# Queries and keys of branch C turned by DMA in two-byte halves instead of by TensorE

## The chip, the cores and the metric

The kernel runs on one core of a Trainium2 chip. The metric is the device time of one execution in microseconds (us), lower is better. All data is float32; every large product is made of three passes over operands split in a high and a low part of type float32r.

## The reference, cut to what matters

Two layers; in each, four token mixers A to D run in parallel on one input projection and are merged through gates. The change lies in mixer C, latent attention with four heads of 128 + 64 features over 512 tokens:

```python
def latent_attention(c_q, c_kv, c_kr, positions, cq_g, w_uq, ckv_g, w_ukv, qn_g, kn_g):
    q = (rms_norm(c_q, cq_g) @ w_uq).reshape(b, s, MLA_HEADS, MLA_QK)      # 128 + 64 per head
    kv = (rms_norm(c_kv, ckv_g) @ w_ukv).reshape(b, s, MLA_HEADS, MLA_NOPE + MLA_V)
    k_nope, v = kv[..., :MLA_NOPE], kv[..., MLA_NOPE:]
    k = concat([k_nope, broadcast(c_kr)])
    q, k = rms_norm(q, qn_g), rms_norm(k, kn_g)
    q, k = (rope applied to the last 64 features of each)
    sc = einsum('bqhd,bkhd->bhqk', q, k) * scale      # contracts over features
    w = softmax(where(chunk mask, sc, NEG_INF));  return w @ v
```

Queries and keys come out of their projections with tokens on the partitions (the norm sums over features there), and the scores need features on the partitions. So both have to be turned: for a pair of heads, six blocks of 128 features x 512 tokens (two heads of keys, two of queries, and one block each in which the 64 rotary features of both heads lie side by side).

## The kernel before, in words

One program per engine, written out by hand, with semaphores between them; each engine runs its instructions strictly in the order of the program. Weights come in chunks of 128 x 1024 float32 through a ring of four slots (`RING = 4`), in the order of the list `ORDER`. SyncE's queue (SP) loads chunk c as soon as chunk c - 4 is used up (`load`, L391 to L397); ScalarE copies it to `w_hi` (`weights_up_to`, L971); GpSimd makes `w_lo` by subtracting (L464, L466); TensorE multiplies (`mm3`, L491 to L493). `project` is 24 matmuls of 512 columns over the eight tiles of the normed input h.

Branch C handles its heads in two pairs per layer (`pair_c(l, p)`, one function on each engine), so there are four such passages in the kernel. `ORDER` has for pair p the chunks kq, gb(d), yb(2p), gb(d+1), gb(d+2), yb(2p+1), gb(d+3), cz, cz with d = 4p. A passage on TensorE is:

1. keys and queries from chunk kq (36 matmuls), `k_ready` and the end of kq are signalled;
2. `gate_b(d)`, `branch_b(d)`: work of branch B, 24 and 12 matmuls, put there as filling;
3. `gate_b(d+1)`, `branch_b(d+1)`. `gate_b(d+1)` writes the bank that `gate_b(d)` wrote, and so first waits for `gb_tanh` of d (L747), which ScalarE signals when its tanh of that bank is done (L1113);
4. 24 transposes of 128 x 128 against the identity (L753 to L765), six banks;
5. `gate_b(d+2)` in bank 6 and `branch_b(d+2)` in bank 7 (L766, L767; the latter waits for `yb_taken` of d+1, from VectorE's L1596);
6. scores (L770), after `t_made` of the last of the six blocks (L769).

ScalarE, in the same passage: squares of keys and queries, `q_tok` copied out of PSUM (L1156), chunk kq+3 to `w_hi`, a square root for the norms (L1161), tanh of `gate_b(d)` (L1162), chunk kq+4, tanh of `gate_b(d+1)`, chunk kq+5, then the six high parts from the turned banks (L1169), chunk kq+6, tanh of `gate_b(d+2)`. VectorE: sums of squares, the rotation of the queries (L1665 to L1669), the scaled keys `k_tok`, `k_rot` (L1675 to L1682, `k_made`), `branch_b(d)` and `branch_b(d+1)` (it takes the bank as a gated value, L1596), six low parts (L1686 to L1691), `branch_b(d+2)`, then the maxima of the scores.

Of the kernel before, what the change touches and what calls it, by code (L numbers as in the profile page):

```python
# [7 lines left out]
F32 = mybir.dt.float32  # L8
F32R = mybir.dt.float32r
BF16 = mybir.dt.bfloat16  # L10
I32 = mybir.dt.int32
ALU = mybir.AluOpType
# [95 lines left out]
def after(n):  # L108

    assert n >= 0  # L110
    return n + 1
# [13 lines left out]
def build(nc, x_in, p_in, pos_in, w_in, par_in, rows_in, const_in, out):  # L125
    ctx = ExitStack()
    with ctx:
# [40 lines left out]
        def plan(start, stop, *items):  # L168
# [44 lines left out]
            *[(n, [SEQ], F32R) for n in ("kr_hi", "kr_lo", "qr_hi", "qr_lo")])  # L213
        k_sq, q_sq = plan(36, 46, ("k_sq", [TB, PAIR, P], F32), ("q_sq", [TB, PAIR, QK], F32))
        k_tok, q_tok, k_rot, q_rot = plan(
            60, 72, ("k_tok", [TB, PAIR, P], F32), ("q_tok", [TB, PAIR, P], F32),
            ("k_rot", [TB, PAIR, 2, HALF], F32), ("q_rot", [TB, PAIR, 2, HALF], F32))
        prob, pt_hi, pt_lo, sz_c, th_b, tmp = plan(
            60, 83, ("prob", [TRI], F32), ("pt_hi", [TRI], F32R), ("pt_lo", [TRI], F32R), ("sz_c", [SEQ], F32),
            ("th_b", [2, SEQ], F32), ("tmp", [SEQ], F32))  # L220
# [35 lines left out]
        def sems(names):  # L256
            return [sem(n) for n in names.split()]
# [27 lines left out]
        t_ready, t_hi_made, t_made = sems("t_ready t_hi_made t_made")  # L285
# [27 lines left out]
        def by_head(t, block):  # L313

            return t.rearrange("p (h t c) -> p h t c", h=G, t=TB)[:, :, block, :]

        def tile(t, i, n=SEQ):

# [70 lines left out]
        @block.sync  # L389
        def _(sync):  # L390
            def load(l, name):  # L391

                c = number(l, name)
                if c >= RING:
                    sync.wait_ge(slot_done[c % RING], c // RING)
                for to, part in gathered(l, name):
                    sync.dma_start(to, part).then_inc(raw_loaded[c % RING], 16)  # L397

            def load_x(d):
                sync.dma_start(tile(x, d), x_in[:, d * SEQ:(d + 1) * SEQ]).then_inc(x_loaded[d], 16)  # L400
# [81 lines left out]
        def _(pe):  # L482
# [230 lines left out]
            def pair_c(l, p):  # L713
# [39 lines left out]
                for b, t_of in enumerate((lambda t: k_tok[:, t, 0, :], lambda t: k_tok[:, t, 1, :],  # L753
                                          lambda t: k_rot[:, t], lambda t: q_tok[:, t, 0, :], lambda t: q_rot[:, t],
                                          lambda t: q_tok[:, t, 1, :])):
                    if p == 0 and b == 4:
                        pe.wait_ge(gb_tanh, after(l * KD + d + 1))
                    if p == 0 and b == 5:
                        pe.wait_ge(yb_taken, after(l * KD + d + 1))
                    for t in range(TB):  # L760
                        i = t_of(t)
                        if b in (2, 4):
                            i = i.rearrange("p h a c -> p (h a c)")
# [198 lines left out]
        def _(act):  # L962
# [180 lines left out]
            def pair_c(l, p):  # L1143
                d, head, n, lp = 4 * p, PAIR * p, l * G + PAIR * p, l * 2 + p
                kq, kb, fill = f"kq{p}", K_BANK[p], 10 - K_BANK[p]
                act.wait_ge(k_ready, after(lp))
                for b in range(2):
                    act.activation(k_sq[:, 2 * b:2 * b + 2].rearrange("p t h c -> p (t h c)"), bank(kb + b),
# [4 lines left out]
                                   ACT.Square).then_inc(q_squared, 1)  # L1153
                act.wait_ge(krr_made, after(l))
                for t in range(TB):
                    last = act.activation(q_tok[:, t], bank(t, PAIR * QK).rearrange("p (h c) -> p h c", h=PAIR)[:, :, 0:P],  # L1156
                                          ACT.Copy)
# [8 lines left out]
                for b, (o, gain) in enumerate(((kn_hi[:, 0], "kn"), (kn_hi[:, 1], "kn"), (kr_hi[:], None),  # L1166
                                               (qn_hi[:, 0], "qn"), (qr_hi[:], None), (qn_hi[:, 1], "qn"))):
                    act.wait_ge(t_ready, after(lp * 6 + b))
                    act.activation(o, bank(b), ACT.Copy, scale=col(l, gain) if gain else 1.0).then_inc(t_hi_made, 1)  # L1169
# [156 lines left out]
        def _(dve):  # L1326
# [319 lines left out]
            def pair_c(l, p):  # L1646
# [26 lines left out]
                dve.tensor_scalar(sm("rq"), sm("qk_inv", 0, 8), Q_SCALE_C, None, ALU.mult)  # L1673
                dve.tensor_scalar(sm("neg_rq"), sm("qk_inv", 0, 8), -Q_SCALE_C, None, ALU.mult)
                for b in range(2):  # L1675
                    dve.tensor_tensor(k_tok[:, 2 * b:2 * b + 2].rearrange("p t h c -> p (t h) c"),
                                      bank(kb + b).rearrange("p (u c) -> p u c", u=4),
                                      over(sm("qk_inv", 8 + 4 * b, 4), [P, 4, P], 2), ALU.mult)
                k_inv = sm("qk_inv", 8, 8).rearrange("p (t h) -> p t h", h=PAIR)
                dve.tensor_tensor(k_rot[:].rearrange("p t h a c -> p t h (a c)"),  # L1680
                                  over(krr[:].rearrange("p t a c -> p t (a c)"), wide, 2), over(k_inv, wide, 3),
                                  ALU.mult).then_inc(k_made, 1)  # L1682
                branch_b(l, d, fill + 1)
                branch_b(l, d + 1, fill + 1)

                for b, (o, h, gain) in enumerate((  # L1686
                        (kn_lo[:, 0], kn_hi[:, 0], "kn"), (kn_lo[:, 1], kn_hi[:, 1], "kn"), (kr_lo[:], kr_hi[:], None),
                        (qn_lo[:, 0], qn_hi[:, 0], "qn"), (qr_lo[:], qr_hi[:], None),
                        (qn_lo[:, 1], qn_hi[:, 1], "qn"))):
                    dve.wait_ge(t_hi_made, after(lp * 6 + b))  # L1690
                    (gained_low(o, bank(b), col(l, gain), h) if gain else low(o, bank(b), h)).then_inc(t_made, 1)  # L1691
                branch_b(l, d + 2, 7)
                maxima(n, 0)
                probabilities(n, 0)
# [274 lines left out]
```

## Time and profile before

| | us |
|---|---|
| median of 3 runs (lowest, highest) | 1358.57 (1358.22, 1361.79) |
| the profiled execution | 1358.55 |
| its span in the trace | 1356.8 |
| busy: TensorE matmul, VectorE, ScalarE, GpSimd | 1350.7, 699.5, 560.5, 606.1 |

The profile is of one execution. Times in it are us from the span's start unless marked ns. PE is TensorE matmul, PEld its weight load, DVE VectorE, ACT ScalarE, POOL GpSimd, SP SyncE. Matmuls are pipelined: a row gives the duration of one matmul, and the time that it costs the engine is the distance to the start of the next. A line such as L493 is the line of the kernel, which can be that of a helper.

### The profile page before, as it was taken

What the parts mean: (1) busy time and instruction counts of PE and PEld (TensorE: products, weight loads), DVE (VectorE), ACT (ScalarE), POOL (GpSimd) and SP (SyncE); (2) the same over time, 40 slices, a digit from 0 to 9 for tenths busy, and PEclk for the clock granted to TensorE, in tenths of its full rate; (3) what the DMA queues carried; (4) which work ended last, traced back from release to release, by engine and by line L of the source; (5) the groups of instructions that cost most, each with busy time, mean ns of one, the idle gap of its engine ahead of it and who ended that gap; (6) DMA issues with size and microseconds to landing.
All of it is one profiled execution on the core that took longest, in us unless ns stands there. A gap on an engine that the chain in (4) does not pass through costs nothing.

```text
span 1356.8 us, 16150 instructions
## 1 busy us (share of the span) xinstructions
PE 1350.7 (100%) x6401; PEld 1136.3 (84%) x6401; DVE 699.5 (52%) x1065; ACT 560.5 (41%) x870; POOL 606.1 (45%) x455
## 2 busy tenths in 40 slices
PE   9999999999999999999999999999999999999998
PEld 8788888888888888888888888888888888888887
DVE  7996445144553223265779955441445432343743
ACT  6365454255552222224444554443555322222242
POOL 3444252444434445445565542334333444544543
PEclk9999999999999999999999999999999999999999
DMA  7322222222222333323333222223222333333332
GB/s 209 92 86 94 63 79 74 90 86 85 87 79 93 93 100 102 109 93 96 99 108 94 85 94 63 78 75 97 78 79 81 90 95 104 97 93 109 100 101 95
DMA packets 68268, 126.32 MB, mean 93 GB/s; under 512 B 9040, under 2 KB 37984, under 8 KB 68192
## 3 DMA queue, kind: packets, MB, share of 16 engines
q1 hardware_dynamic: 66960, 124.72, 30.2%
q8 instruction: 51, 0.84, 0.3%
q10 hardware_dynamic: 1232, 0.55, 0.1%
q14 instruction: 25, 0.20, 0.0%
HBM read 123.15 MB, written 2.10 MB: 92 GB/s over the span
## 4 chain that ended last, share of the span: by engine, by line
PE 98%; DVE 1%; ACT 0%; issue 0%; DVEq 0%
PE ps L491 31%; PE ps L493 31%; PE ps L492 31%; PE ps L764 1%; PE ps L699 1%; PE ps L800 1%; PE ps L686 1%; PE ps L541 1%; PE ps L551 0%; DVE n_t L1453 0%; PE ps L556 0%; DVE h_lo L1336 0%; PE ps L582 0%; DVE r_b L1448 0%; PE ps L618 0%
## 5 line engine op out<-in xcount | busy, mean ns | idle before, releaser
L464 POOL TENSOR_TENSOR w_lo<-w_raw,w_hi 128x512 fp32r<-128x512 f32 x222 | 304.4, 1371 | 724.4 <-ACT w_hi L971 724.3
L491 PE MATMUL ps<-h_hi,w_hi 128*128 128x512 f32 (+1 forms) x1160 | 452.6, 390 | 1.0 <-DVE h_lo L1336 1.0
L493 PE MATMUL ps<-h_hi,w_lo 128*128 128x512 f32 (+1 forms) x1160 | 450.2, 388 | 0.0
L492 PE MATMUL ps<-h_lo,w_hi 128*128 128x512 f32 (+1 forms) x1160 | 449.9, 388 | 0.0
L971 ACT ACTIVATE w_hi<-w_raw 128x1024 fp32r<-128x1024 f32 x227 | 238.6, 1054 | 172.5 <-PE ps L493 166.5
L466 POOL TENSOR_TENSOR w_lo<-w_raw,w_hi 128x512 fp32r<-128x512 f32 x222 | 303.7, 1368 | 0.0
L491 PEld LDWEIGHTS ps<-h_hi,w_hi 128*128 128x128 f32 x1160 | 217.9, 188 | 46.6 <-DVE h_lo L1336 2.6
L493 PEld LDWEIGHTS ps<-h_hi,w_lo 128*128 128x128 f32 x1160 | 217.8, 188 | 45.1
L492 PEld LDWEIGHTS ps<-h_lo,w_hi 128*128 128x128 f32 x1160 | 217.9, 188 | 43.3
L1771 DVE SCALAR_TENSOR_TENSOR m_part<-th,ps 128x512 f32<-128x512 f32 x48 | 33.0, 687 | 237.9 <-PE ps L493 237.7
L1196 ACT ACTIVATE th<-ps 128x512 f32<-128x512 f32 x48 | 28.7, 597 | 183.5 <-PE ps L493 183.5
L491 PE MATMUL ps<-act_hi,w_hi 128*128 128x512 f32 x192 | 75.2, 392 | 0.0
L493 PE MATMUL ps<-act_hi,w_lo 128*128 128x512 f32 x192 | 74.8, 389 | 0.0
L492 PE MATMUL ps<-act_lo,w_hi 128*128 128x512 f32 x192 | 74.7, 389 | 0.0
L491 PE MATMUL ps<-m_hi,w_hi 128*128 128x512 f32 x128 | 49.8, 389 | 0.0
L492 PE MATMUL ps<-m_lo,w_hi 128*128 128x512 f32 x128 | 49.8, 389 | 0.0
L493 PE MATMUL ps<-m_hi,w_lo 128*128 128x512 f32 x128 | 49.8, 389 | 0.0
L493 PEld LDWEIGHTS ps<-act_hi,w_lo 128*128 128x128 f32 x192 | 36.0, 188 | 7.6
L492 PEld LDWEIGHTS ps<-act_lo,w_hi 128*128 128x128 f32 x192 | 36.1, 188 | 7.3
L491 PEld LDWEIGHTS ps<-act_hi,w_hi 128*128 128x128 f32 x192 | 36.1, 188 | 7.3
L1596 DVE SCALAR_TENSOR_TENSOR merged<-th_b,ps 128x512 f32<-128x512 f32 x16 | 11.0, 684 | 50.9 <-PE ps L493 50.9
L491 PE MATMUL ps<-w_hi,act_hi 128*128 128x512 f32 (+1 forms) x96 | 36.9, 384 | 0.0
(329 smaller groups left out, 1992.2 us busy)
## 6 DMA issues: line engine op xcount, KB each, us to landing
w_raw<-w_in SPq DMA_DIRECT2D x180, 512.0 KB, 3.5
w_raw<-w_in SPq DMA_DIRECT2D x92, 128.0 KB, 2.5
w_raw<-w_in SPq DMA_DIRECT2D x36, 256.0 KB, 3.0
x<-x_in SPq DMA_DIRECT2D x8, 256.0 KB, 4.1
w_raw<-w_in SPq DMA_DIRECT2D x32, 64.0 KB, 2.0
out_x<-x SPq DMA_DIRECT2D x7, 256.0 KB, 3.7
p_raw<-p_in SPq DMA_DIRECT2D x2, 512.0 KB, 4.4
w_raw<-w_in ACTq DMA_DIRECT2D x4, 128.0 KB, 3.0
```

What stands on the lines that cost most here:

```text
L464: pool.tensor_tensor(w_lo_t[s][:, 0:4, :], w_raw_t[s][:, 0:4, :], w_hi_t[s][:, 0:4, :].bitcast(F32), ALU.subtract)
L466: pool.tensor_tensor(w_lo_t[s][:, 4:8, :], w_raw_t[s][:, 4:8, :], w_hi_t[s][:, 4:8, :].bitcast(F32), ALU.subtract).then_inc(w_lo_made, 1)
L491: pe.matmul(o, a_hi, b_hi, start=first, stop=False, skip_group_check=skip)
L492: pe.matmul(o, a_hi, b_lo, start=False, stop=False, skip_group_check=skip)
L493: return pe.matmul(o, a_lo, b_hi, start=False, stop=last, skip_group_check=skip)
L541: pe.matmul(bank(t, LAT), act_hi[:, at_[t]], v_hi[:, u, 0:LAT], start=k == 0, stop=False)
L686: last = pe.matmul(ps[:, s:s + keys], q[at_, b * P:keys], k[at_, 0:keys], start=False, stop=q is qr_lo, skip_group_check=True)
L699: last = pe.transpose(ps[:, o:o + P], prob[:, i:i + P], ident[:])
L764: last = pe.transpose(ps[:, b * 512 + t * P:b * 512 + (t + 1) * P], i, ident[:])
L971: act.activation(w_hi_t[s][:, 0:n, :], w_raw_t[s][:, 0:n, :], ACT.Copy).then_inc(w_hi_made, 1)
L1196: act.activation(th[:, i % 4, :], bank(b), ACT.Tanh, scale=0.5).then_inc(g_tanh, 1)
L1771: dve.scalar_tensor_tensor(o, th[:, i % 4, :], 1.0, bank(b), ALU.add, ALU.mult).then_inc(y_taken, 1)
```

## The change

Every block is turned as two planes of two bytes. ScalarE reads a block of float32 as pairs of 16-bit numbers and writes all lower halves and then all upper halves (`split`, 1024 elements per partition); SP issues a DMA transpose of 128 partitions x 1024 two-byte elements from SBUF to SBUF (`turn`); VectorE puts the halves together again (`merge_halves`, 1024 elements). Then the high and low parts are made as before, now from SBUF. The 24 transposes on TensorE and their waits go. The six blocks are taken in the order queries, queries, rotary queries, keys, keys, rotary keys; their instructions stand at new places in the programs of ScalarE, VectorE and SP.

```diff
+        k_half, k_turned, q_half, q_turned, kr_half, kr_turned, qr_half, qr_turned = plan(
+            36, 60, ...)          # the bytes of kn_hi, kn_lo, qn_hi, qn_lo, kr_hi, kr_lo, qr_hi, qr_lo
+        def halves(t):
+            return t.bitcast(U16).rearrange("p (s u) -> p u s", u=2)
+        def planes(t):
+            return t.bitcast(U16).rearrange("p (u s) -> p u s", u=2)
+        TURNED = (q_tok 0, q_tok 1, q_rot, k_tok 0, k_tok 1, k_rot: each with its half and its turned tile)
@@ SyncE
+            def turn(lp, first):
+                for b in range(first, first + 3):
+                    sync.wait_ge(t_split, after(lp * 6 + b))
+                    if b > 2:
+                        sync.wait_ge(t_merged, after(lp * 6 + b - 3))
+                    _, half, turned = TURNED[b]
+                    sync.dma_start_transpose(turned.bitcast(U16).rearrange("p (j s) -> p j s", j=2 * TB),
+                                             half.bitcast(U16)).then_inc(t_turned[b % 3], 16)
...
+                    if name in ("yb1", "gb3", "yb3", "gb7"):
+                        turn(l * 2 + (name in ("yb3", "gb7")), 0 if name.startswith("yb") else 3)
                     if l or not (name.startswith("lat") or name == "av0"):
                         load(l, name)
@@ TensorE, pair_c
-                pe.wait_ge(k_made, after(lp))
-                pe.wait_ge(q_taken, after(lp))
-                pe.wait_ge(q_rotated, after(lp))
-                for b, t_of in enumerate((lambda t: k_tok[:, t, 0, :], ...)):
...
-                    for t in range(TB):
...
-                        last = pe.transpose(ps[:, b * 512 + t * P:b * 512 + (t + 1) * P], i, ident[:])
-                    last.then_inc(t_ready, 1)
@@ ScalarE, pair_c
+                def split(b):
+                    act.activation(planes(TURNED[b][1]), halves(flat_tok(b)), ACT.Copy).then_inc(t_split, 1)
...
                 act.activation(sm("qk_root"), sm("qk_sum"), ACT.Sqrt, bias=eps[:], scale=1.0 / QK).then_inc(qk_root, 1)
+                act.wait_ge(q_taken, after(lp))
+                split(0)
+                split(1)
+                act.wait_ge(q_rotated, after(lp))
+                split(2)
                 gate_b(l, d, fill)
                 weights_up_to(l, kq, 4)
+                act.wait_ge(k_made, after(lp))
+                for b in (3, 4, 5):
+                    split(b)
                 gate_b(l, d + 1, fill)
                 weights_up_to(l, kq, 5)
-                for b, (o, gain) in enumerate((... six blocks, keys first ...)):
-                    act.wait_ge(t_ready, after(lp * 6 + b))
-                    act.activation(o, bank(b), ACT.Copy, scale=...).then_inc(t_hi_made, 1)
+                for b, (o, gain) in enumerate((... six blocks, queries first ...)):
+                    act.wait_ge(t_merged, after(lp * 6 + b))
+                    act.activation(o, flat_tok(b), ACT.Copy, scale=...).then_inc(t_hi_made, 1)
@@ VectorE, pair_c
+                def merge_halves(b):
+                    dve.wait_ge(t_turned[b % 3], 16 * after(lp * 2 + b // 3))
+                    dve.tensor_copy(halves(flat_tok(b)), planes(TURNED[b][2])).then_inc(t_merged, 1)
+                def turned_low(b):
...
+                    dve.wait_ge(t_hi_made, after(lp * 6 + b))
+                    (gained_low(o, flat_tok(b), ...) if gain else low(o, flat_tok(b), h)).then_inc(t_made, 1)
                 branch_b(l, d, fill + 1)
+                for b in range(6):
+                    merge_halves(b)
+                    if b > 2:
+                        turned_low(b - 3)
                 branch_b(l, d + 1, fill + 1)
-                for b, (o, h, gain) in enumerate((... six blocks ...)):
-                    ...low parts from bank(b)...
+                for b in range(3, 6):
+                    turned_low(b)
                 branch_b(l, d + 2, 7)
```

The tiles `q_tok` and `k_tok` are laid out by head and then by token block, so that a block of a head is contiguous; the instructions that write them are otherwise the same.

## Rows read from the trace of the kernel before

**Rows 1.** The page: busy time of the engines, and the chain that ended last.
```profile
PE 1350.7 (100%) x6401; PEld 1136.3 (84%) x6401; DVE 699.5 (52%) x1065; ACT 560.5 (41%) x870; POOL 606.1 (45%) x455
PE 98%; DVE 1%; ACT 0%; issue 0%; DVEq 0%
```

**Rows 2.** Waits of TensorE: waiting line, releaser, us in total, times, longest.
```profile
PE ps L582 <- DVE ones L1384: 1.1, 1, 1.1
PE ps L491 <- DVE h_lo L1336: 1.0, 3, 0.4
```

**Rows 3.** Timeline of TensorE, first passage: start, duration, engine, line, operands, count.
```profile
130.15 1.03 PE L764 MATMUL ps<-ident,k_tok 128*128 128x128 f32 x8
...
132.69 0.47 PE L491 MATMUL ps<-h_hi,w_hi 128*128 128x512 f32 x1
133.00 0.39 PE L492 MATMUL ps<-h_lo,w_hi 128*128 128x512 f32 x1
133.23 0.40 PE L493 MATMUL ps<-h_hi,w_lo 128*128 128x512 f32 x1
```

**Rows 4.** Timeline of ScalarE, first passage: from the square root to the second tanh.
```profile
119.57 0.31 ACT L1161 ACTIVATE small<-small,eps 128x16 f32<-128x16 f32 x1
119.89 1.28 ACT L1113 ACT_TABLE_LOAD   x1
121.19 0.60 ACT L1113 ACTIVATE th_b<-ps 128x512 f32<-128x512 f32 x1
121.68 1.05 ACT L971 ACTIVATE w_hi<-w_raw 128x1024 fp32r<-128x1024 f32 x1
127.63 0.60 ACT L1113 ACTIVATE th_b<-ps 128x512 f32<-128x512 f32 x1 [4.89 <-PE ps L493]
```

**Rows 5.** The same tanh in the three other passages, and two copies in a row.
```profile
184.67 0.60 ACT L1113 ACTIVATE th_b<-ps 128x512 f32<-128x512 f32 x1
792.44 0.60 ACT L1113 ACTIVATE th_b<-ps 128x512 f32<-128x512 f32 x1
839.11 2.03 ACT L971 ACTIVATE w_hi<-w_raw 128x1024 fp32r<-128x1024 f32 x2
855.99 0.60 ACT L1113 ACTIVATE th_b<-ps 128x512 f32<-128x512 f32 x1
```

**Rows 6.** Timeline of TensorE: the first matmul of gate_b(d+1) in each passage.
```profile
121.84 0.50 PE L491 MATMUL ps<-h_hi,w_hi 128*128 128x512 f32 x1
186.05 0.39 PE L491 MATMUL ps<-h_hi,w_hi 128*128 128x512 f32 x1
793.31 0.40 PE L491 MATMUL ps<-h_hi,w_hi 128*128 128x512 f32 x1
857.37 0.39 PE L491 MATMUL ps<-h_hi,w_hi 128*128 128x512 f32 x1
```

**Rows 7.** Timeline of TensorE, first passage: branch_b(d+2) begins, scores begin.
```profile
138.25 0.39 PE L491 MATMUL ps<-act_hi,w_hi 128*128 128x512 f32 x1
140.97 0.39 PE L491 MATMUL ps<-kn_hi,qn_hi 128*128 128x512 f32 x1
```

**Rows 8.** Timeline of VectorE, first passage.
```profile
114.71 1.22 DVE L1650 TENSOR_REDUCE small<-k_sq 128x8 f32<-128x1024 f32 x1 [1.23 <-ACT k_sq L1148]
119.36 0.82 DVE L1669 TENSOR_TENSOR q_rot<-q_rot,q_swap 128x512 f32<-128x512 f32 x1
122.54 0.67 DVE L1680 TENSOR_TENSOR k_rot<-krr,small 128x512 f32<-128x512 f32 x1
132.83 0.68 DVE L1336 TENSOR_TENSOR kr_lo<-ps,kr_hi 128x512 fp32r<-128x512 f32 x1
```

**Rows 9.** The page's DMA issues: KB each, median us from issue to landing.
```profile
w_raw<-w_in SPq DMA_DIRECT2D x36, 256.0 KB, 3.0
out_x<-x SPq DMA_DIRECT2D x7, 256.0 KB, 3.7
```

**Rows 10.** DMA queues from 0 to 12 us: packets, MB, share of 16 engines.
```profile
q10 hardware_dynamic: 1232, 0.55, 16.5%
```

More of the change, by code:

```diff
@@ L11 @@
 I32 = mybir.dt.int32
+U16 = mybir.dt.uint16
 ALU = mybir.AluOpType
@@ L215, in build @@
         k_tok, q_tok, k_rot, q_rot = plan(
-            60, 72, ("k_tok", [TB, PAIR, P], F32), ("q_tok", [TB, PAIR, P], F32),
+            60, 72, ("k_tok", [PAIR, TB, P], F32), ("q_tok", [PAIR, TB, P], F32),
             ("k_rot", [TB, PAIR, 2, HALF], F32), ("q_rot", [TB, PAIR, 2, HALF], F32))
+        k_half, k_turned, q_half, q_turned, kr_half, kr_turned, qr_half, qr_turned = plan(
+            36, 60, *[(n, [PAIR, SEQ], F32) for n in ("k_half", "k_turned", "q_half", "q_turned")],
+            *[(n, [SEQ], F32) for n in ("kr_half", "kr_turned", "qr_half", "qr_turned")])
         prob, pt_hi, pt_lo, sz_c, th_b, tmp = plan(
@@ L284, in build @@
             "k_ready k_squared q_squared q_taken qk_var qk_root k_made q_rotated")
-        t_ready, t_hi_made, t_made = sems("t_ready t_hi_made t_made")
+        t_split, t_merged, t_hi_made, t_made = sems("t_split t_merged t_hi_made t_made")
+        t_turned = [sem(f"t_turned{b}") for b in range(3)]
         s_ready, s_max, exp_made, p_made, pt_ready, pt_hi_made, pt_made, oc_ready, oc_gated, oc_hi_made, act_c_made = sems(
@@ L315, in by_head, with flat_tok @@
             return t.rearrange("p (h t c) -> p h t c", h=G, t=TB)[:, :, block, :]
+        def halves(t):
+            return t.bitcast(U16).rearrange("p (s u) -> p u s", u=2)
+        def planes(t):
+            return t.bitcast(U16).rearrange("p (u s) -> p u s", u=2)
+        TURNED = ((q_tok[:, 0], q_half[:, 0, :], q_turned[:, 0, :]), (q_tok[:, 1], q_half[:, 1, :], q_turned[:, 1, :]),
+                  (q_rot[:], qr_half[:], qr_turned[:]),
+                  (k_tok[:, 0], k_half[:, 0, :], k_turned[:, 0, :]), (k_tok[:, 1], k_half[:, 1, :], k_turned[:, 1, :]),
+                  (k_rot[:], kr_half[:], kr_turned[:]))
+        def flat_tok(b):
+            t = TURNED[b][0]
+            return t.rearrange("p t h a c -> p (t h a c)") if b in (2, 5) else t.rearrange("p t c -> p (t c)")
         def tile(t, i, n=SEQ):
@@ L1155, in pair_c @@
                 for t in range(TB):
-                    last = act.activation(q_tok[:, t], bank(t, PAIR * QK).rearrange("p (h c) -> p h c", h=PAIR)[:, :, 0:P],
+                    last = act.activation(q_tok[:, :, t, :], bank(t, PAIR * QK).rearrange("p (h c) -> p h c", h=PAIR)[:, :, 0:P],
                                           ACT.Copy)
@@ L1161, in pair_c @@
                 act.activation(sm("qk_root"), sm("qk_sum"), ACT.Sqrt, bias=eps[:], scale=1.0 / QK).then_inc(qk_root, 1)
+                act.wait_ge(q_taken, after(lp))
[3 more added lines that the diff above has]
+                split(2)
                 gate_b(l, d, fill)
                 weights_up_to(l, kq, 4)
+                act.wait_ge(k_made, after(lp))
+                for b in (3, 4, 5):
+                    split(b)
                 gate_b(l, d + 1, fill)
                 weights_up_to(l, kq, 5)
-                for b, (o, gain) in enumerate(((kn_hi[:, 0], "kn"), (kn_hi[:, 1], "kn"), (kr_hi[:], None),
-                                               (qn_hi[:, 0], "qn"), (qr_hi[:], None), (qn_hi[:, 1], "qn"))):
-                    act.wait_ge(t_ready, after(lp * 6 + b))
-                    act.activation(o, bank(b), ACT.Copy, scale=col(l, gain) if gain else 1.0).then_inc(t_hi_made, 1)
+                for b, (o, gain) in enumerate(((qn_hi[:, 0], "qn"), (qn_hi[:, 1], "qn"), (qr_hi[:], None),
+                                               (kn_hi[:, 0], "kn"), (kn_hi[:, 1], "kn"), (kr_hi[:], None))):
+                    act.wait_ge(t_merged, after(lp * 6 + b))
+                    act.activation(o, flat_tok(b), ACT.Copy, scale=col(l, gain) if gain else 1.0).then_inc(t_hi_made, 1)
                 weights_up_to(l, kq, 6)
@@ L1675, in pair_c @@
                 for b in range(2):
-                    dve.tensor_tensor(k_tok[:, 2 * b:2 * b + 2].rearrange("p t h c -> p (t h) c"),
-                                      bank(kb + b).rearrange("p (u c) -> p u c", u=4),
-                                      over(sm("qk_inv", 8 + 4 * b, 4), [P, 4, P], 2), ALU.mult)
+                    dve.tensor_tensor(k_tok[:, :, 2 * b:2 * b + 2, :].rearrange("p h t c -> p t h c"),
+                                      bank(kb + b).rearrange("p (t h c) -> p t h c", t=2, h=PAIR),
+                                      over(sm("qk_inv", 8 + 4 * b, 4).rearrange("p (t h) -> p t h", h=PAIR),
+                                           [P, 2, PAIR, P], 3), ALU.mult)
                 k_inv = sm("qk_inv", 8, 8).rearrange("p (t h) -> p t h", h=PAIR)
@@ L1682, in pair_c @@
                                   ALU.mult).then_inc(k_made, 1)
+                def merge_halves(b):
+                    dve.wait_ge(t_turned[b % 3], 16 * after(lp * 2 + b // 3))
+                    dve.tensor_copy(halves(flat_tok(b)), planes(TURNED[b][2])).then_inc(t_merged, 1)
+                def turned_low(b):
+                    o, h, gain = ((qn_lo[:, 0], qn_hi[:, 0], "qn"), (qn_lo[:, 1], qn_hi[:, 1], "qn"),
+                                  (qr_lo[:], qr_hi[:], None), (kn_lo[:, 0], kn_hi[:, 0], "kn"),
+                                  (kn_lo[:, 1], kn_hi[:, 1], "kn"), (kr_lo[:], kr_hi[:], None))[b]
+                    dve.wait_ge(t_hi_made, after(lp * 6 + b))
+                    (gained_low(o, flat_tok(b), col(l, gain), h) if gain else low(o, flat_tok(b), h)).then_inc(t_made, 1)
                 branch_b(l, d, fill + 1)
+                for b in range(6):
+                    merge_halves(b)
+                    if b > 2:
+                        turned_low(b - 3)
                 branch_b(l, d + 1, fill + 1)
[L1686 to L1691, printed above, removed]
+                for b in range(3, 6):
+                    turned_low(b)
                 branch_b(l, d + 2, 7)
```

10 lines of the change are left out of this document (removed).

## The prediction

> **What bounds the kernel now.** I read the page first: TensorE is busy for 1350.7 us of a span of 1356.8, and the chain that ended last lies on it for 98% [rows 1]. Then TensorE's waits: they add up to 2.1 us in two rows, all there are [rows 2]. So every us taken from TensorE's instructions is a us of the end, as long as nothing new makes it wait; and every us that it is made to wait is lost, for no reserve exists. Nothing else in the profile is near. ScalarE is at 41% on average, but the average doesn't say who is late in a passage. So next the timeline of one passage on TensorE, ScalarE and VectorE, and there the place where they meet: `gate_b(d+1)` starts on TensorE at 121.84 [rows 6], and the tanh that frees its bank ends at 121.19 + 0.60 = 121.79 [rows 4]. Its ScalarE program is dense from the square root on: root 119.57 to 119.88, table load to 121.17, tanh 121.19. In this passage ScalarE has 0.05 us to spare, and that is what the change works on.
>
> **What is taken away.** The 24 transposes start at 130.15 and the next product at 132.69: 2.54 us. The first matmul behind them takes 0.31 to the next start (132.69 to 133.00), an ordinary one 0.23 (133.00 to 133.23) [rows 3]: 0.08 more that goes. 2.62 us for each of four passages, 10.5 us, all on the path. The k_made, q_taken and q_rotated waits that go too ended long before (k_made at 123.21 [rows 8] against 130.15) and are worth nothing. The reads of PSUM in the six high and low parts become reads of SBUF: no credit, they are off the path.
>
> **What is added on ScalarE, ahead of the first tanh.** Three splits of 1024 elements. The trace has no copy of two-byte elements. The nearest row is the copy of 1024 four-byte elements: 1.05 us alone, 2.03 for two, so the second adds 0.98 [rows 4, 5]. I take 0.98. Lower bound: 0.49, if what counts are the 512 four-byte words in it. Upper bound: 1.30, a third more, for elements that lie two bytes wide with gaps; no row excludes it. A gain from them is excluded, since they are new instructions on an engine that has no gap there. Three splits: 2.94 us. Their inputs are there: q_rot is ready at 119.36 + 0.82 = 120.18 [rows 8] and the third split would start at 121.84.
>
> So the tanh ends 2.94 us later, and TensorE can start `gate_b(d+1)` at that time plus about 0.05 for the signal (what the first passage shows: 121.79 to 121.84). In the four passages the tanh ended at 121.79, 185.27, 793.04, 856.59 [rows 4, 5] and `gate_b(d+1)` started at 121.84, 186.05, 793.31, 857.37 [rows 6]. New stalls: 121.79 + 2.99 - 121.84 = 2.94; 185.27 + 2.99 - 186.05 = 2.21; 793.04 + 2.99 - 793.31 = 2.72; 856.59 + 2.99 - 857.37 = 2.21. Sum 10.1 us. That eats the gain: -10.5 + 10.1 = -0.4.
>
> **The other three splits** (keys) stand behind the tanh and chunk kq+4. First passage, new times: tanh ends at 124.73, chunk kq+4 to 125.7, k_made long there, splits end at 126.7, 127.7, 128.7. The second tanh waits for the end of gb(d+1), 127.63 + 2.94 = 130.6, so these three lie in a gap that was 4.89 us wide [rows 4]. Free, with 2 us left.
>
> **What is added on VectorE.** Six merges of 1024 elements. The nearest row is the reduction of 1024 elements, 1.22 [rows 8]; I take 1.1 (0.3 to 1.3), 6.6 us. They lie in a gap between branch_b(d) and branch_b(d+1), but now `branch_b(d+1)` stands behind the sixth merge, and TensorE's `branch_b(d+2)` waits for its `yb_taken`.
>
> **The chain through the DMA, and its deadline.** TensorE reached `branch_b(d+2)` at 138.25 and the scores at 140.97 [rows 7]. In the new order, 2.62 earlier by the transposes and 2.94 later by the stall: 138.6 and 141.3. Call T5 the landing of the sixth transfer. Then the merge (1.1), a low part (0.65; a row of this kind has 0.68 [rows 8]) and branch_b(d+1) (0.7): yb_taken at T5 + 2.5. So T5 has to be at most 136.1. The scores need two or three more low parts, T5 + 4.5, within 2.7 us of the product between: they are not the tighter one. Two paths lead to T5. From the keys: the last split ends at 128.7, which leaves 7.4 us for one transfer. From the queries: turn(3 to 5) each wait for the merge of the block three before, whose transfer starts no earlier than 120.9, 121.9, 122.9 (splits of the queries); with a transfer of L us, T5 = 122.9 + L + 1.1 + L, which is in time up to L = 6.0. And if the transfers run one after another, s us each, T5 = 120.9 + 6 s, in time up to s = 2.5.
>
> No row shows a transpose by DMA. The nearest rows are ordinary transfers of the same 256 KB: 3.0 us to land into SBUF, 3.7 out of it [rows 9], and transfers of SP overlap. By these L is 3 to 4 and the chain is hidden, at no cost. The other bound comes from small pieces: 1232 packets took 16.5% of 16 engines for 12 us, 25.7 ns each [rows 10]. One block has 1024 runs of 256 bytes; as packets, 64 on each engine, 1.6 us. If the turning cuts runs eight times finer, to 32 bytes, it is 13 us for each transfer. A gain is excluded. I take the value next to the 256 KB rows, hidden, with the weaker confidence that this deserves.
>
> The Trainium skill (VectorE: DVE Perf Modes, The three transpose paths) has 1309 ns for a 128 x 128 block by the DMA crossbar against 390 ns on TensorE, and advises TensorE where PSUM will do as the destination. Taken as a rate, eight blocks in a transfer make 10.5 us and T5 = 183.9, an estimate from that page that would cost 48 us per passage; as a time that mostly isn't rate, nothing changes. The same skill (DMA: Bandwidth & Descriptors, Latency and other measured facts) has 261 GB/s for DMA transposes, 1.0 us for a block. The two pages disagree tenfold; no row here decides.
>
> **SP's queue.** The turns stand ahead of the loads of yb(2p+1) and gb(d+3). The first was issued at 119.1 as soon as gb(d) was used up; now it waits for the third split, 122.9. It must be landed, copied (1.05) and subtracted (2.5) by `branch_b(d+2)`, 138.6: landed by 135.0, with 3.1 for the load issued by 131.9. Nine us of slack; free if a turn holds SP for under 3 us. gb(d+3) must wait for yb(2p) to be used up (about 133.1) in any case; turn(5) has passed before.
>
> **Sum.** 1358.55 (the profiled execution, 0.02 below the median of 1358.57; its span 1356.8 and 1.75 around it) - 10.5 + 10.1 + 0 = 1358.2. With splits at 1.30 it is +3.9 = 1362.1; at 0.49, 3 x 0.49 less per passage, 5.9 less = 1352.3.
>
> **Rivals.**
> - *The chain is late by a few us.* The transfers run one after another at 3.0 us [rows 9]: T5 = 138.9, 2.8 us late in each passage, 11 us: 1369. It decides from s = 2.5 on. For it: all six are issued by one queue, and each of the last three waits for a merge three before it. Against: ordinary transfers overlap. This is the case that ends slower; it covers 1362 to 1382.
> - *Transposing by DMA is slow in itself*, the page's first figure or pieces of 32 bytes. At 5 us each T5 = 150.9, 14.8 us late, 59 us: 1417. At 13 us, 200.4, 64 us late: 1615. For it: two-byte elements are scattered across partitions. Against: nothing in the trace, which shows no such operation.
> - *Splits are cheap*, 0.49 each: 1352, faster. For it: the bytes are half those of the copy. Against: ScalarE's rows scale with elements, 0.60 for 512 and 1.05 for 1024 [rows 4].
>
> **How the numbers follow.** Chain hidden, splits at 0.9 to 1.3: 0.40, 1354 to 1362, forecast 1358. Cheap splits: 0.11. Chain late by up to 6 us a passage: 0.28. Slow transposes: 0.21. What this measurement can tell from no change is about 0.3%, 4.1 us. Faster by more 0.11, within 0.40, slower by more 0.49. The range: from the cheap splits' time, 1352, with half of that case left out below it, up to 1400, which takes a third of the slow case and leaves out 0.14. More likely than not the result isn't faster, though the single likeliest time is no change.
>
> **What the profile would show.** Right: no L764; a new wait of TensorE at L491 for ScalarE's th_b, four times, 2.2 to 2.9 us; the split rows at about 1.0 us; VectorE's merges started before 135 in the first passage; no wait for yb_taken or t_made. The late chain: TensorE waits for `merged` (VectorE) ahead of `branch_b(d+2)`, and VectorE's merge for the DMA. Slow transposes: the same with tens of us, SP blocked, and w_hi waiting for DMA. What would make it wrong: a transfer over 6 us or a split far from 1 us, or a lower granted clock of TensorE behind the new pauses.

## The result and the profile after

| | us | ratio to before, 95% interval |
|---|---|---|
| before, median of 4 runs (lowest, highest) | 1359.08 (1358.22, 1361.79) | |
| the change, median of 4 runs | 1366.79 (1364.94, 1366.99) | 1.0052 (1.0037 to 1.0067) |
| spans of the profiled executions | 1356.8 and 1364.9 | |

The change is slower by half a per cent. The forecast of no change was wrong: 1358 was forecast and 1366.8 measured, inside the stated range (1352 to 1400) and above the 4.1 us that the prediction still took for no change.

The page of the changed kernel, its busy times and the chain that ended last (answers to rows 1):

```profile
PE 1345.8 (99%) x6305; PEld 1128.5 (83%) x6305; DVE 739.4 (54%) x1089; ACT 584.3 (43%) x894; POOL 613.0 (45%) x455
PE 89%; DVE 6%; ACT 4%; issue 0%; DVEq 0%
```

96 transposes (24 in each of four passages) are gone, but TensorE's busy time fell by 4.9 us only, not by 10.5: matmuls elsewhere took longer. And 10% of the chain now lies on VectorE and ScalarE. TensorE's waits (answers to rows 2; waiting line, releaser, us in total, times, longest):

```profile
PE ps L526 <- ACT th_b L1132: 9.1, 4, 2.7
PE ps L526 <- DVE kr_lo L1367: 3.8, 4, 1.0
PE ps L617 <- DVE ones L1415: 1.1, 1, 1.1
PE ps L526 <- DVE h_lo L1367: 1.0, 3, 0.4
```

The first is the wait for the tanh that the prediction worked out. The second is new to it: the scores wait for the last low part. Next the timelines of the first passage, ScalarE, then VectorE, then SP's transposes (they answer to rows 4 and 8):

```profile
119.89 0.31 ACT L1184 ACTIVATE small<-small,eps 128x16 f32<-128x16 f32 x1
120.10 1.99 ACT L1167 ACTIVATE q_half<-q_tok 128x1024 uint16<-128x1024 uint16 x2
122.00 1.04 ACT L1167 ACTIVATE qr_half<-q_rot 128x1024 uint16<-128x1024 uint16 x1
123.06 1.28 ACT L1132 ACT_TABLE_LOAD   x1
124.35 0.60 ACT L1132 ACTIVATE th_b<-ps 128x512 f32<-128x512 f32 x1
...
132.39 0.60 ACT L1132 ACTIVATE th_b<-ps 128x512 f32<-128x512 f32 x1 [3.66 <-PE ps L528]
132.88 1.05 ACT L990 ACTIVATE w_hi<-w_raw 128x1024 fp32r<-128x1024 f32 x1
133.83 1.33 ACT L1200 ACTIVATE qn_hi<-q_tok,par 128x512 fp32r<-128x512 f32 x2
```
```profile
131.49 0.76 DVE L1718 COPY k_tok<-k_turned 128x1024 uint16<-128x1024 uint16 x1 [1.71 <-DMA k_turned<-k_half]
134.58 1.29 DVE L1371 SCALAR_TENSOR_TENSOR qn_lo<-q_tok,par,qn_hi 128x512 fp32r<-128x512 f32 x1 [2.33 <-ACT qn_hi L1200]
135.79 1.84 DVE L1718 COPY k_tok<-k_turned 128x1024 uint16<-128x1024 uint16 x1
...
139.41 0.67 DVE L1627 SCALAR_TENSOR_TENSOR merged<-th_b,ps 128x512 f32<-128x512 f32 x1
140.01 2.45 DVE L1371 SCALAR_TENSOR_TENSOR kn_lo<-k_tok,par,kn_hi 128x512 fp32r<-128x512 f32 x2
142.38 1.77 DVE L1367 TENSOR_TENSOR kr_lo<-k_rot,kr_hi 128x512 fp32r<-128x512 f32 x1
```
```profile
q_turned<-q_half SPq DMA_TRANSPOSE x8, 3.3
k_turned<-k_half SPq DMA_TRANSPOSE x8, 3.9
qr_turned<-qr_half SPq DMA_TRANSPOSE x4, 3.2
kr_turned<-kr_half SPq DMA_TRANSPOSE x4, 3.2
```

(The last four are from the page's DMA issues: count, median us to landing.) The splits cost what they were given, 1.99 for two and 1.04 for one. The DMA lands in 3.2 to 3.9 us, like an ordinary transfer of 256 KB [rows 9]. VectorE is where the surprise is: from 134.58 on it has no gap until the low part that the scores wait for is done at 144.15, and its rows are up to 2.6 times as long as the row of the same line and tile in rows 8 (1.77 against 0.68). GpSimd subtracts at the same time, and the rows of the two engines take turns:

```profile
134.01 1.30 POOL L499 TENSOR_TENSOR w_lo<-w_raw,w_hi 128x512 fp32r<-128x512 f32 x1 [4.85 <-ACT w_hi L990]
135.26 1.76 POOL L501 TENSOR_TENSOR w_lo<-w_raw,w_hi 128x512 fp32r<-128x512 f32 x1
```

VectorE's low part of 134.58 ends at 135.87, some 0.6 us behind the end of GpSimd's first row (135.31). GpSimd's second row ends 1.15 us behind that (137.02), and VectorE's merge of 135.79 ends 0.6 us behind GpSimd (137.63).

Third, the clock. Stretches of the first passage on TensorE, with the granted clock behind the busy times (stretch, length, busy time and count of PE, PEld, DVE, ACT, POOL, clock, DMA share, GB/s):

```profile
119.40:125.00 5.60, 2.86 (x13) 2.05 (x11) 4.09 (x9) 5.56 (x8) 2.25 (x2) 1.00 0.47 89
125.00:129.00 4.00, 4.00 (x11) 3.14 (x12) 4.00 (x4) 3.73 (x4) 3.03 (x2) 0.57 0.80 208
129.00:132.20 3.20, 3.20 (x16) 2.62 (x15) 1.49 (x2) 0.00 (x0) 0.16 (x1) 1.00 1.20 199
```

For 4 us behind the pause of 2.74 us the granted clock was 0.57, in the main the lower of its two levels (1.2 GHz instead of 2.4), and a matmul of 512 columns came every 0.43 us instead of 0.23.

Counted from one start to the next on TensorE's timeline, the four passages (from the start of `gate_b(d)` to the start of the scores) went like this:

| passage | before | after | `branch_b(d)` and pause | `gate_b(d+1)` | second pause |
|---|---|---|---|---|---|
| 1 | 27.39 | 30.31 | 2.72 + 2.90 | 7.19 | 1.14 |
| 2 | 27.16 | 27.90 | 2.72 + 2.10 | 5.58 | 1.12 |
| 3 | 27.18 | 30.03 | 2.72 + 2.64 | 7.18 | 1.13 |
| 4 | 27.16 | 27.89 | 2.72 + 2.11 | 5.57 | 1.13 |

Ordinary durations are 2.72 for 12 matmuls and 5.44 to 5.59 for 24. So: -10.5 for the transposes, +9.8 for the first pauses, +3.2 for the slow clock (7.19 and 7.18 against 5.58), +4.5 for the second pauses and +0.5 for the first matmul of the scores behind them (0.12 four times), 7.5 together. The spans differ by 8.1. Another 0.3 is the first matmul behind the pauses of passages 2 and 4 (`gate_b(d+1)` took 5.58 and 5.57 there, 5.44 before), and 0.3 arose ahead of the first passage.

### The profile page after: what moved, and what is told of

Same layout as the page of the kernel before. It is cut to its first block, busy times and chain, and to the rows that moved or that the text cites. A ratio compares the mean times of both kernels' runs of the same rounds, so it can differ in the third digit from the quotient of the medians.

```text
span 1364.9 us, 16038 instructions
## 1 busy us (share of the span) xinstructions
PE 1345.8 (99%) x6305; PEld 1128.5 (83%) x6305; DVE 739.4 (54%) x1089; ACT 584.3 (43%) x894; POOL 613.0 (45%) x455
## 3 DMA queue, kind: packets, MB, share of 16 engines
q1 hardware_dynamic: 92304, 131.02, 32.5%
## 4 chain that ended last, share of the span: by engine, by line
PE 89%; DVE 6%; ACT 4%; issue 0%; DVEq 0%
PE ps L526 28%; PE ps L528 28%; PE ps L527 28%; DVE kn_lo L1371 1%; ACT w_hi L990 1%; PE ps L734 1%; PE ps L819 1%; PE ps L721 1%; DVE k_tok L1718 1%; DVE qn_lo L1371 1%; DVE kr_lo L1367 0%; PE ps L576 0%; PE ps L586 0%; ACT q_sq L1175 0%; DVE n_t L1484 0%; ACT q_half L1167 0%
## 5 line engine op out<-in xcount | busy, mean ns | idle before, releaser
L499 POOL TENSOR_TENSOR w_lo<-w_raw,w_hi 128x512 fp32r<-128x512 f32 x222 | 306.2, 1379 | 725.5 <-ACT w_hi L990 725.4
L501 POOL TENSOR_TENSOR w_lo<-w_raw,w_hi 128x512 fp32r<-128x512 f32 x222 | 309.2, 1393 | 0.0
L1141 ACT ACTIVATE prob<-ps,small 128x512 f32<-128x512 f32 (+3 forms) x32 | 19.5, 614 | 44.9 <-DVE small L1644 44.9
L1315 ACT ACTIVATE o_sq<-x 128x512 f32<-128x512 f32 x16 | 10.1, 634 | 64.0 <-DVE x L1843 64.0
```

Source lines behind the costliest of these rows:

```text
L499: pool.tensor_tensor(w_lo_t[s][:, 0:4, :], w_raw_t[s][:, 0:4, :], w_hi_t[s][:, 0:4, :].bitcast(F32), ALU.subtract)
L501: pool.tensor_tensor(w_lo_t[s][:, 4:8, :], w_raw_t[s][:, 4:8, :], w_hi_t[s][:, 4:8, :].bitcast(F32), ALU.subtract).then_inc(w_lo_made, 1)
L1141: last = act.activation(prob[:, s], ps[:, sc + s.start:sc + s.stop], ACT.Exp, bias=sm("bias", h * TB + b), scale=sm("rq", b * PAIR + h), a ...
```

## The experiments

**Theory 1**: the time is lost in the order of the instructions on ScalarE and VectorE. The splits ahead of the first tanh hold up TensorE, the pause takes its clock down, and VectorE's chain of merges and low parts, lengthened by GpSimd, ends late. The DMA is not a cause. **Theory 2**, in its variants: the transposing DMA is slow or disturbs the loads; or one engine's order alone is the cause.

### The DMA replaced: e1_plain_copy

```diff
-                    sync.dma_start_transpose(turned.bitcast(U16).rearrange("p (j s) -> p j s", j=2 * TB), half.bitcast(U16))
+                    sync.dma_start(turned.bitcast(U16), half.bitcast(U16))
```

> The changed kernel, with each of its 24 DMA transposes replaced by a plain DMA copy of the same 256 KB (so queries and keys are not turned, and the scores are other numbers). Theory 1, the time is lost in the order of ScalarE and VectorE and not in the DMA: the profile of the changed kernel has TensorE wait 9.1 us for the tanh and 3.8 us for the last low part, and VectorE waits only 5.1 us for the DMA, ahead of a wait for ScalarE that ends later anyway. So no change: 1366.8, within 2 us, and the same two waits of TensorE. Theory 2, the crossbar is slow or disturbs the loads of the weights: the second wait goes and the time falls by 4 to 8 us, to 1359 to 1363.

Measured: 1365.51 (ratio to before 1.0046, 1.0031 to 1.0061), the same two waits of TensorE to the tenth of a us:

```profile
PE ps L525 <- ACT th_b L1131: 9.1, 4, 2.7
PE ps L525 <- DVE kr_lo L1366: 3.8, 4, 1.0
```

The plain copies were quicker: they landed in 2.2 to 2.4 us and held SP's queue for 0.47 us each, against 3.1 to 5.0 and 1.2 to 2.1 us for the transposes, and VectorE's 5.1 us of waits for `k_turned` are gone. The time can't be told apart from the changed kernel's all the same. So that these transfers transpose is not the cause. The transfers themselves and their place in SP's queue are still there in this run; e9 changes the order in that queue.

### The splits alone: e2_three_splits and e3_two_splits

```diff
                 act.activation(sm("qk_root"), ...).then_inc(qk_root, 1)
+                act.wait_ge(q_taken, after(lp))
+                act.wait_ge(q_rotated, after(lp))
+                for to, t in (...three blocks...)[0:3]:          # e3: [0:2]
+                    act.activation(to as two planes, t as two-byte halves, ACT.Copy)
                 gate_b(l, d, fill)
```

> The kernel before with three splits of 1024 two-byte elements on ScalarE ahead of the first tanh of a passage, and nothing else of the change: their result is not used. Theory 1: TensorE waits for the tanh in each of the four passages, 2.9 + 2.2 + 2.7 + 2.2 = 10.0 us, and behind the two longer waits its granted clock falls for some 4 us, 1.7 us each, as the trace of the changed kernel has it at 125 us: 1359.1 + 10.0 + 3.4 = 1372.5. If the clock fell for the DMA traffic or the work of VectorE and not for the wait, it stays up here: 1369.1. Theory 2: the same wait, no word on the clock.

> The kernel before with two such splits. Waits of 1.95 + 1.2 + 1.75 + 1.2 = 6.1 us. If the clock falls only behind a longer wait, as in the changed kernel behind 2.7 us and not behind 2.1 us, the granted clock stays full: 1359.1 + 6.1 = 1365.2. If any new wait made it fall, 1.7 us more for each of four: 1372.

Measured: 1377.08 (1.0132, 1.0115 to 1.0149) with three, 1368.03 (1.0063, 1.0048 to 1.0078) with two. TensorE's waits for the tanh were 11.1 and 7.3 us. They are longer than expected because my edit waits for the rotated queries ahead of all splits (ScalarE stood 0.39 us there), and because a pause costs some 0.2 us more than the wait row says, from the end of one matmul stream to the next. The rest is the clock. Two stretches of 4 us of e2, directly behind two of its pauses:

```profile
192.20:196.20 4.00, 3.94 (x10) 3.12 (x11) 0.69 (x1) 0.95 (x2) 2.51 (x2) 0.57 0.00 0
125.40:129.40 4.00, 3.98 (x17) 3.29 (x18) 0.68 (x1) 0.91 (x1) 2.54 (x2) 1.00 0.02 4
```

This kernel transposes on TensorE and moves nothing extra by DMA, and it has the slow clock too: behind three of its four pauses, `gate_b(d+1)` took 7.18, 8.31 and 7.21 us instead of 5.6. So the slow clock comes with the pauses, and it needs neither DMA traffic (0.00 in the slow stretch) nor VectorE's added work. But which pause is not settled by its length: here the longest, 3.23 us, kept the full clock and one of 2.44 did not; in e3 one of 2.29 did not and one of 2.02 did. The expectation that e3 would stay clear of it was wrong (one drop). The whole price of the three splits ahead of the tanh, as measured here, is 18.5 us.

### What could be had at most: e4_no_turning

The transposes are left out on TensorE, ScalarE waits for `k_made`, `q_taken` and `q_rotated` in their stead.

> The kernel before with the 24 transposes of a passage left out on TensorE: the high and low parts are made of what lies in the banks, so the scores are other numbers. It measures what the change could bring at most on TensorE. By the rows of before, 4 x 2.62 = 10.5 us: 1348.6. If the wait for the scores' operands became visible once the cover of 2.62 us is gone, less, some 1350 to 1353.

Measured: 1348.14 (0.992, 0.9905 to 0.9935), 10.5 us below the 1358.61 of before in the same session. The gain on TensorE was rated right. That it fits to the tenth is luck in part: the interval of the ratio allows 8.8 to 12.9 us.

### The queries' splits behind the tanh: e5_splits_behind

```diff
-                split(0); split(1); wait q_rotated; split(2)
                 gate_b(l, d, fill)
                 weights_up_to(l, kq, 4)
+                split(0); split(1); wait q_rotated; split(2)
                 act.wait_ge(k_made, after(lp))
```

> The changed kernel with one move on ScalarE: the three splits of the queries stand behind the first tanh and chunk kq+4 instead of ahead of them. Theory 1: the wait of TensorE for the tanh (10.0 us with its restarts) and the slow clock behind two of them (3.3 us) go; but then TensorE comes to branch_b(d+2) 2.6 us earlier than in the kernel before, while VectorE takes branch_b(d+1) only behind six merges, and those come with the DMA 1 to 2 us later than now. By adding up its rows yb_taken comes some 3.4 us late in each passage: 1358.6 - 10.5 + 13.6 = 1361.7, 1358 to 1366, and the wait is for VectorE's merged. Theory 2, the order of ScalarE is the whole cause: 1366.8 - 13.3 = 1353.5.

Measured: 1374.26 (1.011, 1.0096 to 1.0124), slower than the change. Both theories missed. The wait for the tanh is gone, as said, and the wait for `merged` is there, as theory 1 said, but it is 16.2 us:

```profile
PE ps L526 <- DVE merged L1627: 16.2, 4, 4.9
PE ps L526 <- DVE kr_lo L1367: 1.0, 1, 1.0
```

I had added up VectorE's rows and left out the other engine that feeds them. ScalarE, first passage:

```profile
128.90 0.58 ACT L1132 ACTIVATE th_b<-ps 128x512 f32<-128x512 f32 x1
132.64 1.06 ACT L990 ACTIVATE w_hi<-w_raw 128x1024 fp32r<-128x1024 f32 x1 [3.16 <-DMA w_raw<-w_in]
133.61 1.32 ACT L1200 ACTIVATE qn_hi<-q_tok,par 128x512 fp32r<-128x512 f32 x2
```

The chunk yb(2p+1) is loaded behind three turns in SP's queue, the turns now start at 124.3, and ScalarE stands 3.16 us for it ahead of the high parts. The pauses then bring the clock down as well: behind those of 4.17, 3.55 and 4.94 us the 12 matmuls of `branch_b(d+2)` took 4.19, 4.35 and 4.73 us instead of 2.72, with granted clocks of 0.64, 0.64 and 0.50 in the first 4 us. Behind the fourth, 3.59 us, the clock stayed at 1.00.

### VectorE without GpSimd beside it: e6_pool_quiet

```diff
+                    if name[0:2] in ("gb", "yb", "cz"):
+                        pool.memset(w_lo_t[s][:].bitcast(F32), 0.0).then_inc(w_lo_made, 1)
+                        continue
```

> The changed kernel, but for the weight chunks gb, yb and cz GpSimd writes zeros for the low part instead of subtracting two tiles (so the low parts of these weights are left out of the result). Theory 1, VectorE's merges and low parts, which now read only SBUF, are held up by GpSimd: the rows of 1.2 to 1.85 us become 0.7 to 0.8, the last low part is ready some 3 us earlier and the second wait of TensorE (4.6 us with its restarts) goes: 1362. Theory 2, these operations are slow by themselves or the second wait is only a matter of order: rows and time as now, 1366.8.

Measured: 1360.36 (1.0016, 1.0007 to 1.0025). VectorE in the first passage, the same instructions as above:

```profile
132.37 0.75 DVE L1374 SCALAR_TENSOR_TENSOR qn_lo<-q_tok,par,qn_hi 128x512 fp32r<-128x512 f32 x1 [1.29 <-ACT qn_hi L1203]
133.04 0.76 DVE L1721 COPY k_tok<-k_turned 128x1024 uint16<-128x1024 uint16 x1
...
136.16 1.42 DVE L1374 SCALAR_TENSOR_TENSOR kn_lo<-k_tok,par,kn_hi 128x512 fp32r<-128x512 f32 x2
137.49 0.70 DVE L1370 TENSOR_TENSOR kr_lo<-k_rot,kr_hi 128x512 fp32r<-128x512 f32 x1
```

1.29, 1.84, 2.45 and 1.77 have become 0.75, 0.76, 1.42 and 0.70, and the second wait is gone. So an operation of VectorE that reads and writes SBUF alone is slowed by GpSimd's subtractions at the same time. One with an operand in PSUM is not: `merged` took 0.67 at 123.14 in the kernel before, all of it inside GpSimd's row of 122.81 to 124.36. (The 0.68 of rows 8 doesn't show it, since GpSimd stood idle from 131.77 to 135.21.) GpSimd is not fully quiet in e6 either: it still writes zeros, 0.95 us a chunk. Where this met merges both grew, the low parts beside it did not (0.75 at 196.01 beside zeros of 195.43, 0.69 at 201.14 beside those of 201.30):

```profile
189.01 1.92 POOL L498 MEMSET w_lo<- 128x1024 f32 x1 [6.37 <-ACT w_hi L993]
190.06 1.48 DVE L1721 COPY q_rot<-qr_turned 128x1024 uint16<-128x1024 uint16 x1
```

The kernel also saved about 1.3 us of the first pauses and part of the slow clock, which was not expected of it: its square root came 0.8 and 0.5 us earlier against TensorE in passages 1 and 3.

### Orders put together: e7, e8, e9, e10

e7_behind_order is e5 with one more move, on VectorE:

```diff
                 for b in range(6):
+                    if b == 3:
+                        branch_b(l, d + 1, fill + 1)
                     merge_halves(b)
                     if b > 2:
                         turned_low(b - 3)
-                branch_b(l, d + 1, fill + 1)
```

e8_turns_after_load is e7 with one more move, on SP:

```diff
-                    if name in ("yb1", "gb3", "yb3", "gb7"):
-                        turn(l * 2 + (name in ("yb3", "gb7")), 0 if name.startswith("yb") else 3)
+                    if name in ("gb3", "gb7"):
+                        turn(l * 2 + (name == "gb7"), 0)
+                        turn(l * 2 + (name == "gb7"), 3)
```

e9 is the changed kernel with SP's move alone, e10 is e8 without VectorE's.

> As e5_splits_behind, and VectorE takes branch_b(d+1) ahead of the fourth merge instead of behind the sixth. Theory 1: the wait for yb_taken goes, and what is late is the last low part, by 1 to 2.5 us in each passage: 1358.6 - 10.5 + 4 to 10 = 1352 to 1358. Theory 2: as e5_splits_behind, 1353.5.

> As e7_behind_order, and SP issues the load of chunk yb(2p+1) before the first DMA transpose instead of behind the third. Theory 1: the chunk lands some 5 us earlier, ScalarE is not held up by it ahead of the high parts, and the last low part is late by 0 to 1 us: 1348.5 to 1353, the best of these. Theory 2: nothing hangs on the loads, the same as e7_behind_order.

> The changed kernel with one move on SP alone: the load of chunk yb(2p+1) stands ahead of the first DMA transpose instead of behind the third. In the changed kernel ScalarE takes that chunk at 132.88, behind the second tanh, and the chunk is there by then; so theory 1 expects no change, 1366.8 within 1.5, although the same move was worth 12 us once the splits stood behind the tanh. Theory 2, loads held up by the transposes already cost here: 1361 to 1364.

> As e8_turns_after_load, but VectorE takes branch_b(d+1) where the change puts it, behind the sixth merge. By e8's rows that is at 138.0 in the first passage, 1.7 us after TensorE wants the bank (136.22); with the restart 1.9 us for each of four, less the 0.4 us that the scores waited in two passages of e8: 1350.1 + 6 to 7 = 1356.5, and TensorE waits for merged. If VectorE's order were no cause: 1350.1.

| splits behind the tanh | branch_b(d+1) ahead | load ahead of the turns | kernel | us | ratio to before (95%) |
|---|---|---|---|---|---|
| | | | the change | 1366.79 | 1.0052 (1.0037 to 1.0067) |
| | | x | e9 | 1365.91 | 1.0053 (1.0036 to 1.0069) |
| x | | | e5 | 1374.26 | 1.011 (1.0096 to 1.0124) |
| x | x | | e7 | 1362.16 | 1.0022 (1.0012 to 1.0032) |
| x | | x | e10 | 1359.37 | 1.0002 (0.9992 to 1.0011) |
| x | x | x | e8 | 1350.08 | 0.9934 (0.9922 to 0.9947) |

e8 is 8.6 us faster than the kernel before, and 1.9 us from the kernel that turns nothing at all (e4, 1348.14), where the intervals of the two ratios overlap. The move of `branch_b(d+1)` was not run with the splits ahead of the tanh, so its worth there is not known. All waits of TensorE in e8:

```profile
PE ps L618 <- DVE ones L1416: 1.1, 1, 1.1
PE ps L527 <- DVE h_lo L1368: 1.0, 3, 0.4
PE ps L527 <- DVE kr_lo L1368: 0.9, 2, 0.6
```

e9 came out as theory 1 had it: SP's order costs nothing as long as ScalarE is late by itself. The same move is worth 12.1 us from e7 to e8, as against 3.5 to 5 expected. e7 missed its expectation (1352 to 1358) by the same chunk: ScalarE waits 3.27 us for it ahead of the high parts, and TensorE now waits for GpSimd's part of that chunk too (2.5 us). e10 was expected at 1356.5 and came at 1359.37: the wait for `merged` is there (5.3 us in four, as against 7.6 expected), the scores still wait in two passages for 2.1 us, and its runs lie 4 us apart. e7, e10 and e6 spread over 4 us or more where the kernel before spreads over 2 to 4 and e8 over 0.8. The mean granted clocks of the single runs go along with it: e7's fastest (1359.82) had 1.0 and those at 1364.11 and 1363.98 had 0.997 and 0.996; e10's at 1361.32 and 1360.94 had 0.997, those at 1358.14 and 1358.33 had 1.0, though its fastest, 1357.09, had 0.999; e8's five all had 1.0, and e5's 0.990 to 0.994. That the spread is the number of drops a run meets fits this in the main. It is not shown, for only one run of each kernel has a trace.

## Why the prediction was wrong, point by point

- **What bounds the kernel, the gain of 10.5.** Right; e4 measured 10.5.
- **Splits at 0.98, the late tanh, 10.1 us of stalls.** Right: 0.95 to 1.0 each in a row (1.04 alone), stalls of 2.90, 2.10, 2.64 and 2.11, 9.8 us. The first pauses were forecast one by one, within 0.11 us each. The cheap splits (0.49) are refuted: ScalarE takes as long for 1024 elements of two bytes (1.04) as of four (1.05).
- **The transfers.** No row of before showed them, and the value taken, that of ordinary transfers, was right: 3.2 to 3.9 us, 1.2 to 1.4 us of SP's queue each. A plain copy between the same tiles landed in 2.3 us (e1), so the transposing costs about 1 us on top. The pieces of 32 bytes are refuted: SP's queue moved 92,304 packets instead of 66,960, 1056 for each transpose, near the 1024 runs of 256 bytes. (The rival of 13 us was added up wrongly: 120.9 + 6 x 13 is 198.9, 62.8 us late and 1609, not 200.4, 64 and 1615.) T5 was kept too: the sixth transpose of the first passage was issued at 130.37 and landed at most 5.0 us later, 135.4 against 136.1, but VectorE merged it only at 138.18. Of the two pages of the Trainium skill, the time of 1309 ns (VectorE: DVE Perf Modes, The three transpose paths) is no rate for eight blocks one after another: 10.5 us would have been needed where 3.3 were. The rival that ends slower has the right time, 1362 to 1382, and the wrong mechanism: the chain is late by VectorE, not by serial transfers, and TensorE waits ahead of the scores, not for `merged` ahead of `branch_b(d+2)`.
- **"The reads of PSUM become reads of SBUF: no credit, they are off the path".** This is the step that failed. No credit was given, but no charge either. I priced low parts at 0.65 to 0.7 from a row that reads PSUM, and the merges at 1.1, 1.3 at most. Measured: merges 0.75 alone and up to 1.85 beside GpSimd, low parts 0.7 and up to 1.8. In the first passage the last low part was ready 11.76 us behind the start of the second tanh (132.39 to 144.15), where TensorE left 10.68 (to 143.07, the scores without their pause). In e6 the same chain took 8.01 us (130.18 to 138.19) with the same 10.68 to spend. The trace of before had the spread, in the rows of the same line by operands (duration ns lowest/median/highest):

```profile
L1336 DVE TENSOR_TENSOR h_lo<-n_t,h_hi x16: 679/685/1781, 44.1 to 726.7; 128x512 fp32r<-128x512 f32 x16
L1336 DVE TENSOR_TENSOR kr_lo<-ps,kr_hi x4: 677/678/680, 132.8 to 868.2; 128x512 fp32r<-128x512 f32 x4
L1336 DVE TENSOR_TENSOR act_lo<-ps,act_hi x32: 673/690/693, 89.0 to 1059.9; 128x512 fp32r<-128x512 f32 x32
```

  The same subtraction, both operands in SBUF against one in PSUM: 679 to 1781 (1781 beside GpSimd's row of 50.26), and 677 to 680 or 673 to 693. Of the two rows from PSUM it is `act_lo` that tells something, since one of its 32 ran beside GpSimd (100.65, 0.69); `kr_lo` ran in gaps of GpSimd. Read so, the bound for a low part out of SBUF would have been 0.68 to 1.78.
  The Trainium skill states the rule behind these rows (SBUF — State Buffer, "SBUF: two separate sides"): VectorE and GpSimd share one pair of ports, which an instruction of VectorE in a 2-port mode, or with two inputs in SBUF (these only against a GpSimd instruction that reads SBUF), and an instruction of GpSimd hold in turn, for the whole instruction, while the other waits. The traces agree: 1.29, 1.84, 2.45 (two rows) and 1.77 in the change against 0.75, 0.76, 1.42 and 0.70 in e6, surpluses of 0.54, 1.08, 1.03 and 1.07 us, each less than one GpSimd instruction (1.29); the rows that take turns from 134.01 on; and e6, where low parts ran beside GpSimd's zeros, which read nothing, at full speed. It is the rule that spoke against this change, and the prediction didn't weigh it.
- **The deadline of the scores.** "They are not the tighter one" was wrong. `yb_taken` came at 140.08 and TensorE wanted it at 140.35; it was the scores that waited 1.1 us. Besides the longer rows, one edge of the chain was left out: the first low part needs its high part, which stands behind the second tanh and chunk kq+5 on ScalarE, and that tanh waits for TensorE. VectorE stood 2.33 us for it, up to 134.58. This edge alone doesn't make the scores wait: the pause and the slow clock move the tanh and the scores alike, and in e6 the chain behind the tanh fits with 2.7 us to spare. Nor did the forecast profile hold: it had no wait for t_made, and the second wait of TensorE is one.
- **The clock** was named as a thing that could make the forecast wrong, without a price. It had one, 1.6 us behind each of two pauses, 3.2 in all, where the sum had nothing.
- **SP's queue, "nine us of slack".** Right for the kernel as changed (e9), and no longer once the splits stand later (e5, e7).

The sum in the prediction's own terms: -10.5 as forecast, +9.8 for +10.1, and 0 for what measured +5.0 (VectorE's chain) and +3.2 (clock). Its net of -0.4 became +7.5. So two terms failed that stood at nothing: the charge for VectorE's operands in SBUF, and the clock.

## What to carry to other kernels

When an operand moves from PSUM to SBUF, price VectorE's operations again, by rows with both operands in SBUF and at the times when GpSimd works, not by the row of the same line. A stall worked out for an engine is not the end of the sum: carry it on through the instructions that wait for that engine (here the second tanh, the high parts, the low parts), and give the clock behind it a price. And a change that removes work from the bounding engine can be right in idea and lose by three positions in programs: the same instructions in another order were 16.7 us apart (1366.79 and 1350.08), and moves of which one looked harmful alone (+7.5 us for e5) and one useless (about 0 for e9) made that together with a third, which was not run alone.

## What the runs showed of the hardware

- A DMA transpose of 128 x 1024 two-byte elements from SBUF to SBUF lands in 3.2 to 3.9 us (median by tile; 3.1 to 5.0 over all) with 1.2 to 1.4 us in SP's queue (2.1 at most). A plain copy between the same tiles lands in 2.2 to 2.4 us with 0.47 us in the queue (e1), and moves the same bytes in 144 packets instead of 1056. So the transpose costs some 1 us more to landing and 0.8 us more of the queue; in this kernel neither changed a wait of TensorE.
- VectorE copies 1024 two-byte elements from SBUF to SBUF in 0.75 us when GpSimd is quiet, and in up to 1.85 us beside GpSimd's subtraction. GpSimd pays too: its row of 1.29 us becomes up to 1.77 (L501 in the changed kernel) and 1.78 (L502 in e8).
- Behind a pause of TensorE at `gate_b(d+1)` the granted clock fell to 0.57 for some 4 us in 10 of 24 cases (the change, e1, e2, e3, e6, e9, four each): in 9 of 11 pauses of 2.29 to 3.23 us, in 1 of 11 pauses of 1.9 to 2.1 us and in neither of two of 1.5. Each cost 1.5 to 2.7 us; behind the drop of 2.7 us the clock was at 0.50 and 0.55 for 6 us (e2). At other places e5 had three drops behind four pauses of 3.55 to 4.94 us, e7 one behind four of 1.33 to 1.95 at the scores, e10 one behind 1.97 at `branch_b(d+2)`, and the change, e1 and e9 none behind twelve of 0.94 to 0.96. What decides between two pauses of equal length (2.74 us in the change and in e9, the first with the drop, the second without) stays open.
